# RetNet decoder step: states decayed in place on ScalarE, V's outer product added by halves on VectorE

## What is computed

```python
lg = retention_log_decay()                       # per head
inner = jnp.einsum('bhnm,bhme->bhne', scores, v)
cross = jnp.einsum('bhnd,bhde->bhne', q, s_prev) * cross_decay
kv = jnp.einsum('bhmd,bhme->bhde', k * k_decay, v)
s_new = jnp.exp(log_gamma * L) * s_prev + kv     # L = 1 for the decode tokens
```

## Time and profile before

| | us |
|---|---|
| median of 3 runs | 1504.73 (1503.93 to 1508.87) |
| the profiled execution's own time | 1507.03 |
| its span in the profile | 1505.2 |
| TensorE busy in the span | 1483.4 (99%) |
| VectorE busy | 767.7 (51%) |
| ScalarE busy | 512.6 (34%) |
| mean granted clock of TensorE | 0.997 of full speed |

### The profile page before, as it was taken

How to read it: one execution, slowest core, us unless ns; L and a number is a source line. 1 busy time by engine, 2 the same in 40 slices (tenths; PEclk the granted TensorE clock), 3 DMA queues, 4 the chain that set the end, 5 groups by cost and what they waited for, 6 DMA issues and landing times.

```text
span 1505.2 us, 27424 instructions
## 1 busy us (share of the span) xinstructions
PE 1483.4 (99%) x11530; PEld 1407.5 (94%) x11530; DVE 767.7 (51%) x1020; ACT 512.6 (34%) x709; POOL 2.0 (0%) x20
## 2 busy tenths in 40 slices
PE   8999999999999999999999999999999999999998
PEld 8689859968986999999999999999999999999997
DVE  7556347435634785555553325444565555554222
ACT  5252144126215553333332313222333333333222
POOL 0000000000000000000000000000000000000000
PEclk9999999999999999999999999999999999999999
DMA  6533352353345222222222232222322222222221
GB/s 235 211 154 123 145 202 95 124 205 159 116 149 207 105 98 98 84 97 84 89 92 92 82 99 94 87 99 85 99 86 87 96 85 96 84 98 89 97 85 57
DMA packets 47439, 171.87 MB, mean 114 GB/s; under 512 B 5440, under 2 KB 5824, under 8 KB 46320
## 3 DMA queue, kind: packets, MB, share of 16 engines
q1 hardware_dynamic: 47360, 170.71, 32.6%
HBM read 149.35 MB, written 21.55 MB: 114 GB/s over the span
## 4 chain that ended last, share of the span: by engine, by line
PE 94%; DMA 3%; DVE 1%; ACT 1%; issue 0%; SPq 0%; DVEq 0%; ACTq 0%
PE ps L371 82%; PE ps L493 3%; DMA w_raw<-in_w_units_dram 3%; PE ps L536 2%; PE ps L566 2%; PE ps L546 1%; PE ps L561 1%; PE ps L528 1%; PE ps L404 1%; DVE w_lo L996 1%; PE ps L520 1%; ACT w_hi L762 0%; PE ps L473 0%; PE ps L573 0%; DMA model_consts<-in_model_consts_dram 0%
## 5 line engine op out<-in xcount | busy, mean ns | idle before, releaser
L762 ACT ACTIVATE w_hi<-w_raw 128x1024 fp32r<-128x1024 f32 x227 | 240.1, 1060 | 781.4 <-PE ps L371 635.8
L371 PE MATMUL ps<-h_hi,w_hi 128*128 128x264 f32 (+2 forms) x2304 | 471.2, 286 | 6.7 <-DVE h_lo L1021 6.7
L996 DVE TENSOR_TENSOR w_lo<-w_raw,w_hi 128x1024 fp32r<-128x1024 f32 x227 | 277.0, 1222 | 377.3 <-ACT w_hi L762 376.9
L371 PE MATMUL ps<-h_lo,w_hi 128*128 128x264 f32 (+2 forms) x2304 | 468.4, 285 | 0.0
L371 PE MATMUL ps<-h_hi,w_lo 128*128 128x264 f32 (+2 forms) x2304 | 467.2, 284 | 0.0
L371 PEld LDWEIGHTS ps<-h_hi,w_hi 128*128 128x128 f32 x2304 | 357.6, 189 | 7.3 <-issue 6.6
L371 PEld LDWEIGHTS ps<-h_hi,w_lo 128*128 128x128 f32 x2304 | 357.4, 189 | 0.0
L371 PEld LDWEIGHTS ps<-h_lo,w_hi 128*128 128x128 f32 x2304 | 357.3, 189 | 0.0
L371 PE MATMUL ps<-z_hi,w_lo 128*128 128x264 f32 (+1 forms) x832 | 167.9, 283 | 0.0
L371 PE MATMUL ps<-z_lo,w_hi 128*128 128x264 f32 (+1 forms) x832 | 167.8, 283 | 0.0
L371 PE MATMUL ps<-z_hi,w_hi 128*128 128x264 f32 (+1 forms) x832 | 167.5, 283 | 0.0
(11 more groups left out here) (168 smaller groups left out, 1237.2 us busy)
## 6 DMA issues: line engine op xcount, KB each, us to landing
w_raw<-in_w_units_dram SPq DMA_DIRECT2D x227, 512.0 KB, 3.3
states<-in_state_ret_dram SPq DMA_DIRECT2D x32, 512.0 KB, 6.8
out_ret_s_dram<-states SPq DMA_DIRECT2D x32, 512.0 KB, 2.6
v_bcast<-v_scratch SPq DMA_DIRECT2D x8, 1024.0 KB, 5.7
x_res<-in_x_all_dram SPq DMA_DIRECT2D x8, 268.0 KB, 4.5
out_ret_p_dram<-tmp SPq DMA_DIRECT2D x4, 512.0 KB, 4.5
out_y_prompt_dram<-y_rows SPq DMA_DIRECT2D x4, 512.0 KB
decay<-in_decay_dram SPq DMA_DIRECT2D x4, 279.0 KB, 4.0
```

The source lines that it names most:

```text
L371: out = mm(PS[:, 2 * s + half, at:at + n_col], a, b[:, lo:lo + n_col], start=first and n == 0, stop=last and n == 2)
L762: fn(WH[:, c % NS, :], RAW[:, c % NR, :], ACT.Copy).then_inc(hi_ready, 1)
L996: tt(WL[:, c % NS, :], RAW[:, c % NR, :], WH[:, c % NS, :].bitcast(F32), ALU.subtract).then_inc(lo_ready, 1)
```

## The change

ScalarE no longer forms outer products. `outer(b)` is gone; `decay_state(b)` multiplies all 1024 elements of state b by the head's decay, in place. VectorE's `update(b)` now adds the outer product itself: for each half one operation of 512 elements, V's broadcast row times the key's scalar plus the half. `G` is no longer used for this, so ScalarE doesn't wait for `s_upd` any more; the wait for the broadcast V goes from ScalarE to VectorE. The places of the calls change on ScalarE alone: nothing ahead of the copy of the prompt state, state 0 to 3 ahead of the four block copies, states 4 to 7 behind the last one. The line numbers of everything behind fall by 8.

```diff
--- before.py
+++ after.py
@@ -179,7 +179,7 @@
         hi_ready = sem("hi_ready")
         h_hi, h_sq, rstd, rows_rstd = sem("h_hi_ready"), sem("h_sq"), sem("rstd"), sem("rows_rstd")
         v_ready, kn_ready, kv_ready = sem("v_ready"), sem("kn_ready"), sem("kv_ready")
-        samp_kv, o_ready, os_ready = sem("samp_kv"), sem("o_ready"), sem("os_ready")
+        s_decayed, o_ready, os_ready = sem("s_decayed"), sem("o_ready"), sem("os_ready")
         o_sq, g_std, g_silu, z_hi = sem("o_sq"), sem("g_std"), sem("g_silu"), sem("ret_z_hi_ready")
         conv_some, ff_silu, ff_hi = sem("conv_some"), sem("ff_silu"), sem("ff_hi")
         end_act, warm, y_ready = sem("end_act"), sem("warm"), sem("y_ready")
@@ -826,29 +826,21 @@
                     src = PS[0:mn, (6, 6, 7, 7, 1)[j], (j % 2) * DK:(j % 2 + 1) * DK]
                     fn(KN[0:mn, j, :], src, ACT.Copy, scale=DEC[0:mn, TP + j:TP + j + 1]).then_inc(kn_ready, 1)
 
-                def outer(b):
-
-                    if b in (0, NB // 2):
-                        act.wait_ge(vb_in[b // (NB // 2)], 16 * h + 16)
-                    if b >= 2:
-                        act.wait_ge(s_upd, 8 * h + (b - 1))
-                    for e in range(2):
-                        at = (b % 2) * 1024 + e * DV
-                        fn(G[:, at:at + DV], VB[:, b, :], ACT.Copy, scale=KD8[:, e, b:b + 1]).then_inc(samp_kv, 1)
-
-                outer(0)
-                outer(1)
+                def decay_state(b):
+
+                    fn(S[:, b, :], S[:, b, :], ACT.Copy, scale=DEC[:, TP + 5:TP + 6]).then_inc(s_decayed, 1)
+
                 act.wait_ge(kv_done, h + 1)
                 fn(KV, PS[:, 6:8, :].rearrange("p e v -> p (e v)"), ACT.Copy).then_inc(kv_ready, 1)
                 act.wait_ge(samp_done, h + 1)
                 fn(OS[:], PS[:, 1, :], ACT.Copy).then_inc(os_ready, 1)
                 for dt in range(4):
-                    outer(dt + 2)
+                    decay_state(dt)
                     act.wait_ge(inner_done, 4 * h + (dt + 1))
                     at = 1024 * INNER[dt] + CUT
                     fn(O[:, dt, :], PS[:].rearrange("p b n -> p (b n)")[:, at:at + T], ACT.Copy).then_inc(o_ready, 1)
-                outer(6)
-                outer(7)
+                for b in range(4, NB):
+                    decay_state(b)
                 split_hi(8 + NS, U_HEAD, h)
                 act.wait_ge(kv_sent, 16 * h + 16)
                 for dt in range(4):
@@ -1153,12 +1145,13 @@
                         tt(acc, O[:, 0, cols] if dt == 1 else acc, O[:, dt, cols], ALU.add).then_inc(o_sum, 1)
 
                 def update(b):
-                    if b == 0:
-                        dve.wait_ge(samp_done, h + 1)
-                    dve.wait_ge(s_in[b], 16 * h + 16)
-                    dve.wait_ge(samp_kv, 16 * h + (2 * b + 2))
-                    at = (b % 2) * 1024
-                    stt(S[:, b, :], S[:, b, :], DEC[:, TP + 5:TP + 6], G[:, at:at + 1024], ALU.mult, ALU.add).then_inc(s_upd, 1)
+                    if b % 4 == 0:
+                        dve.wait_ge(vb_in[b // 4], 16 * h + 16)
+                    dve.wait_ge(s_decayed, NB * h + b + 1)
+                    for e in range(2):
+                        part = S[:, b, e * DV:(e + 1) * DV]
+                        out = stt(part, VB[:, b, :], KD8[:, e, b:b + 1], part, ALU.mult, ALU.add)
+                    out.then_inc(s_upd, 1)
 
                 for b in range(5):
                     update(b)
```

## The result

| | before | with the change |
|---|---|---|
| median | 1504.73 us (1502.80 to 1508.87, 11 runs) | 1510.25 us (1507.86 to 1512.82, 11 runs) |
| ratio, 95% interval | | 1.0038 [1.0029, 1.0046] |
| profiled execution, its span | 1507.03, 1505.2 us | 1507.86, 1506.1 us |

The change makes the kernel 5.5 us slower; the interval is 4.4 to 6.9 us. Forecast were +4.5 us and 1509.2, and the measured time is in the range. In what follows one thing about the profiled executions matters: the one of before happens to lie in the upper part of its runs, the one of after is the fastest of its eleven. So the two spans, only 0.9 us apart, can't be subtracted to read the effect. What can be compared is the time between two instructions of one head.

What follows compares the result with a forecast made beforehand. TensorE, busy 1483.4 us, was taken as the bound. Two late deliveries, 4 x (0.89 + 0.19) = 4.3 us, plus 0.2 for restarts gave +4.5 us on 1504.7: 1509.2 us, range 1505.5 to 1511.7.

Steps and rivals of the forecast that it cites:

- First delivery: Channel sum for TensorE's averaging matmul: comes later behind state 4's decay and halves, 0.89 us lost in each head.
- restart loss: TensorE restarts with a weight load that isn't overlapped: up to 0.1 us per head, 0.2 us taken in all.
- Second delivery: Last gate read, ahead of the output projection's second pair: delayed by halved updates, 0.19 us lost in each head.
- a small wait: New TensorE wait of 0.2 us at the output projection, expected in the changed kernel.
- What costs nothing: ScalarE's lighter work, VectorE's wait for V, later stores and unchanged DMA count: no time won or lost.
- relief: ScalarE's copy without the wait for V releases TensorE earlier: 1 us per head gives 1500.7; chance 0.05, including other gains.
- Sum: Four heads of 0.89 + 0.19 us make 4.3, plus 0.2 for restarts: +4.5 us, 1509.2 us.
- Paid back: Shorter TensorE waits for next heads' weight units return heads 0 to 2's loss: 1.1 us remains, 1505.8; chance 0.12.
- The halves don't overlap: Each half update holds VectorE its whole 744 ns: 1.56 us a head, 6.2 us, 1510.9; chance 0.13.

Runs made afterwards that it cites:

- both delays taken away: Changed kernel with ScalarE's decays one step earlier and VectorE's updates of states 6 and 7 right behind state 5's: 1505.99 us, 1.0005 of the kernel before.
- the run with one pair more: Changed kernel with VectorE's update of state 5 also ahead of the channel sum: 1518.59 us, 1.0089 of the kernel before.
- the run with spread loads: Kernel with both delays taken away, its loads of states 4 to 7 one each behind weight units 7, 8, 9 and 10: 1517.99 us, 1.0089 of the kernel before.

## Why the prediction was right, and how far

- **First delivery, 0.89 us a head.** It measured 0.91 to 0.93 in A. The terms were read again: decay 1.14 us (I took 1.145), the gap to VectorE 225.00 + 1.14 to 226.24, 0.10 (0.11), the pair of halves 1.33 (1.33), the sum from 227.57 to 230.14 + 0.37 = 230.51, 2.94 (2.89). The average's weight load came 0.92 us later in head 2, counted from the scores (362.01 - 326.71 = 35.30, before 362.20 - 327.82 = 34.38), and A grew by 0.91. So the restart loss, which I put at up to 0.1 us and took as 0.05 without a row for it, is not seen beside the delay of the load.
- **Second delivery, 0.19 us a head.** B grew by 0.2 to 0.23. The halving alone in the kernel before gives the same B. The forecast comes this near partly by luck, since two of its details are wrong. I took 0.03 us from the gate read's end to TensorE's weight load. The load at 254.45 comes 0.12 behind the read's end (253.63 + 0.70 = 254.33), and before it came 0.11 behind it, so there was hardly any slack where I counted 0.08. And 0.07 us are lost already at the start of the output projection, which waits for the low part of block 0 of z; I had named that wait and not priced it. The low part is done at 250.54 + 0.70 = 251.24, and the load at 251.36 is again 0.12 behind it. The second place adds only the rest of the delay, 0.2 us. No wait is listed for either in the waits of TensorE; the steps of the weight loads and the length of the chain's stretch show them. I had said a small wait would be seen; that sign was badly chosen.
- **What costs nothing.** ScalarE's wait for V is gone, its relief won nothing, and with both delays taken away the kernel is at 1.0005 [0.9994, 1.0016].
- **Sum.** 4.6 us from the lengths against 4.5 forecast. The median says 5.5, with 4.4 to 6.9 as its interval, and 1.0027 [1.0011, 1.0043] when taken again. The 0.9 us between lengths and median are inside the interval. The mean granted clock gives no sign that the change makes falls more frequent: 0.9975 and 0.9975 over its 11 and 6 runs, 0.9974 to 0.9979 over the three sets of runs of the kernel before.
- **Paid back** (0.12) is refuted by the run with one pair more: 1.32 us were added to each head and TensorE's wait ahead of the scores stayed at 6.7 us.
- **The halves don't overlap** (0.13): two halves took 1.41 us from start to end against 2 x 0.747, and four 2.73. The rule of the Trainium skill, "VectorE: DVE Perf Modes", section "The DRAIN you can't avoid", that the next operation doesn't start until the pipeline is empty, is not what these rows show: each starts some 0.08 us before the end of the last. The same section of the Trainium skill adds that a next operation that is not held starts earlier, which I left out; the rows agree with that. The rule of the Trainium skill in the same page's section "Rules for kernel authors", to keep the number of operations low, holds here in its direction, for 0.2 us a head.
- **What I passed over.** I took the wait ahead of the scores as a constant and blamed the queue of state loads. The run with spread loads shows that the transfers do matter there, but the larger and simpler part was the engines' order, in plain sight in the chain before: the values' scaling stood behind the splitting of units that weren't needed yet. And I took the spread between runs as noise, where the waits and the falls of the granted clock behind them explain much of it.

## What to carry to other kernels

When an operation is moved in an engine's hand-written order, ask what stands behind it in the queue, here a channel sum that TensorE waits for, and how long the next-needed result has been ready: 3.1 us of slack were given away by a call placed two blocks later, and the price of the operation itself hardly mattered. Delays of TensorE, busy 99% of the span, added up one for one here, and they are read best as the distance between two instructions of the chain, not from spans of single executions. Where the bounding engine waits, look first whether the result it needs stands behind work that nobody needs yet.

## What the runs showed of the hardware that I had not expected

A wait of TensorE can cost more than its length. Behind waits of 1.9 to 2.4 us ahead of the scores, in some executions and not in others, the granted clock was 0.50 for some 3.3 us, 1.2 in the place of 2.4 GHz, and about 1.65 us were lost on top. In these profiles no fall was seen in a head behind a shorter wait. The length of the wait alone doesn't decide it: there was no fall behind one of 2.7 us, nor behind three of four waits of 2.0 us at the average. Behind those of 2.6 to 3.5 us of the run with spread loads it fell in each head. With these waits gone, the times of a kernel lie within 0.5 to 1.6 us (five runs each); with them, mostly within 3 to 9. The exceptions are the run with one pair more, 2.3 us, and the one with spread loads, 1.1 us, of four runs each.

Two operations of VectorE in a row overlap by some 0.08 us here (1.41 us for two halves of 0.747). And TensorE doesn't always start equally soon behind the result that it waits for: the averages' weight load started 0.04 us behind the last addition of the channel sum (361.79 + 0.18 to 362.01 in head 2), the two loads in the output projection 0.12 behind VectorE's operation. What makes the difference stays open.
